# Attention steps in the order turnings, values, masks, scores, with the masks opening the sums

## What is computed

```python
def masked_softmax(s, mask):
    s = jnp.where(mask, s, -jnp.inf)
    m = jnp.max(s, axis=-1, keepdims=True)
    ...
    e = jnp.where(mask, jnp.exp(s - m), 0.0)
    d = jnp.sum(e, axis=-1, keepdims=True)
    return e / jnp.where(d > 0, d, 1.0)
...
    s = jnp.einsum('bqhd,bshd->bhqs', qb, k, preferred_element_type=jnp.float32) * scale
    s = s + (cq[..., :, None] - cum[..., None, :])
    p = masked_softmax(s, kpos[None, :] <= tpos[:, None])
    return jnp.einsum('bhqs,bshd->bqhd', p.astype(v.dtype), v)
```

## Time and profile before

| | |
|---|---|
| median of three runs | 2459.36 us |
| the profiled execution | 2456.09 us |
| its span | 2454.3 us |
| mean granted clock of TensorE | 0.992 |
| TensorE matmuls busy | 2387.1 us, 97% |
| TensorE weight loads busy | 1924.0 us, 78% |
| VectorE busy | 1423.9 us, 58% |
| ScalarE busy | 1019.7 us, 42% |
| GpSimd busy | 274.1 us, 11% |
| chain of waits, by engine | PE 84%, VectorE 7%, issue 5%, ScalarE 3% |

### The profile page before, as it was taken

One profiled execution on the slowest core, in us unless ns is written; L12 is line 12 of the kernel. 1 busy time (PEld: TensorE's weight loads), 2 busy tenths in 40 slices (PEclk: granted clock), 3 DMA queues, 4 the chain that ended last, 5 costly groups with the idle time before them and its releaser, 6 DMA issues.

```text
span 2454.3 us, 32007 instructions
## 1 busy us (share of the span) xinstructions
PE 2387.1 (97%) x12074; PEld 1924.0 (78%) x12086; DVE 1423.9 (58%) x2366; ACT 1019.7 (42%) x1732; POOL 274.1 (11%) x260
## 2 busy tenths in 40 slices
PE   8999899999999999999999999999999999999998
PEld 7877788888887888788888866777888777678886
DVE  3545655655655666566556469947533578676333
ACT  3656654322334444443233334444422354445223
POOL 0000111000000000100000236302100233011001
PEclk9999999999999999999999999999999999999999
DMA  5211002433432111133433312111222221102321
GB/s 196 95 52 44 2 27 95 155 132 117 154 120 95 61 52 61 52 120 132 148 124 137 113 65 73 60 35 36 95 95 95 78 78 61 44 27 78 103 95 52
DMA packets 58039, 211.77 MB, mean 86 GB/s; under 512 B 6432, under 2 KB 6560, under 8 KB 57888
## 3 DMA queue, kind: packets, MB, share of 16 engines
q1 hardware_dynamic: 57456, 208.86, 24.9%
q10 hardware_dynamic: 432, 0.85, 0.1%
HBM read 207.60 MB, written 2.10 MB: 85 GB/s over the span
## 4 chain that ended last, share of the span: by engine, by line
PE 84%; DVE 7%; issue 5%; ACT 3%; POOL 1%; DMA 0%; SPq 0%; ACTq 0%; DVEq 0%; POOLq 0%
PE bank L458 76%; PE last_bank L458 5%; PE bank L468 3%; DVE arena L1145 1%; DVE arena L2232 1%; DVE arena L2234 1%; DVE small L831 1%; ACT arena L819 1%; ACT wparts L566 0%; POOL rstd L625 0%; DMA cb_sb<-cb_dram 0%; DVE arena L2219 0%; DVE arena_r L584 0%; DVE wparts L570 0%; DVE arena L2216 0%
## 5 line engine op out<-in xcount | busy, mean ns | idle before, releaser
L458 PE MATMUL bank<-hT,wparts 128*128 128x512 f32 x5520 | 1330.9, 397 | 5.7 <-DMA cb_sb<-cb_dram 3.5
L458 PEld LDWEIGHTS bank<-hT,wparts 128*128 128x128 f32 x5520 | 1030.4, 189 | 236.5 <-issue 23.2
L570 DVE TENSOR_TENSOR wparts<-ring,wparts 128x1024 fp32r<-128x1024 f32 x290 | 366.8, 1265 | 427.0 <-ACT wparts L566 426.8
L458 PE MATMUL bank<-arena_r,wparts 128*128 128x512 f32 x2400 | 564.0, 395 | 0.0
L458 PEld LDWEIGHTS bank<-arena_r,wparts 128*128 128x128 f32 x2400 | 449.8, 188 | 106.6 <-DVE arena_r L600 0.5
L566 ACT ACTIVATE wparts<-ring 128x1024 fp32r<-128x1024 f32 x332 | 348.2, 1049 | 164.0 <-PE bank L458 131.0
L819 ACT ACTIVATE arena<-bank,small 128x128 f32<-128x128 f32 (+3 forms) x192 | 101.1, 527 | 143.5 <-DVE small L831 142.3
L468 PE MATMUL bank<-cf_sb,arena 128*128 128x128 f32 (+1 forms) x816 | 133.4, 282 | 14.6 <-DMA cf_sb<-cf_dram 4.8
L458 PE MATMUL last_bank<-arena 128*128 128x64 f32 x972 | 131.5, 271 | 8.6 <-DVE arena L854 4.8
L458 PEld LDWEIGHTS last_bank<-arena 128*128 128x128 f32 x972 | 122.6, 193 | 17.5 <-issue 11.3
L831 DVE TENSOR_REDUCE small<-bank 128x1 f32<-128x128 f32 (+3 forms) x192 | 93.4, 486 | 57.1 <-PE bank L458 45.4
(11 more groups left out here) (277 smaller groups left out, 2122.8 us busy)
## 6 DMA issues: line engine op xcount, KB each, us to landing
ring<-weights_dram SPq DMA_DIRECT2D x388, 512.0 KB, 3.4
arena<-x_dram SPq DMA_DIRECT2D x4, 512.0 KB, 5.7
out_dram<-arena SPq DMA_DIRECT2D x4, 512.0 KB, 3.9
rot<-rot_dram SPq DMA_DIRECT2D x1, 512.0 KB, 10.5
rot<-rot_dram ACTq DMA_DIRECT2D x1, 512.0 KB, 3.3
cf_sb<-cf_dram SPq DMA_DIRECT2D x1, 416.0 KB, 8.9
cb_sb<-cb_dram SPq DMA_DIRECT2D x1, 264.0 KB, 9.8
vecs<-vec_dram ACTq DMA_DIRECT2D x1, 258.5 KB, 5.9
```

Of the source, the lines that this page charges most:

```text
L458: i = pe.matmul(*args, **kw)
L570: eng.tensor_tensor(wparts[:, slot, 1, :, :], ring[:, p % RAW, :, :], wparts[:, slot, 0, :, :].bitcast(F32), ALU.subtract)\
```

## The change

In `softmax_maps` TensorE's step i now does, in this order: the turning of map i-3, the values of map i-4, the masks of map i, the scores of map i. The first mask opens the sum (`start=True`), the scores are added to it and the last of them ends it and signals it. A mask of 128 columns opens a sum that is up to 512 wide. Steps are M+4 in place of M+3; ScalarE's and VectorE's copies of the turned map are those of map i-3, VectorE's output that of map i-4. Maximum, exponentials, reciprocal and gate keep their offsets. Within each engine's step, ScalarE, VectorE and GpSimd keep their order. In "fox" the two masks change places, so that the causal one comes first. Pools and lists of numbers stay as they are.

```diff
             def pe_part(pe):
                 for w in ready:
                     pe.wait_ge(*w)
-                for i in range(M + 3):
-                    if i < M and (not together or i % 2 == 0):
...
-                        for j, bank in zip(both, taken):
-                            m = maps[j]
-                            for n, (q, k) in enumerate(m["qk"]):
-                                mm(pe, bank[:, 0:m["width"]], lhsT=q, rhs=k, start=n == 0, stop=False)
-                        for j, bank in zip(both, taken):
-                            extra = maps[j]["masks"]
-                            for n, (a, b, c, w) in enumerate(extra):
-                                for wt in w:
-                                    pe.wait_ge(*wt)
-                                mm(pe, bank[:, c:c + b.shape[-1]], lhsT=a, rhs=b, start=False, stop=n == len(extra) - 1,
-                                   done=(key, "s", j) if n == len(extra) - 1 else None)
-                    if 2 <= i < M + 2:
-                        j = i - 2
+                for i in range(M + 4):
+                    if 3 <= i < M + 3:
+                        j = i - 3
...
-                    if i >= 3:
-                        j = i - 3
+                    if i >= 4:
+                        j = i - 4
...
+                    if i < M and (not together or i % 2 == 0):
...
+                        taken = [banks.take(pe, (key, "s", j), two) for j in both]
+                        for j, bank in zip(both, taken):
+                            for n, (a, b, c, w) in enumerate(maps[j]["masks"]):
+                                for wt in w:
+                                    pe.wait_ge(*wt)
+                                mm(pe, bank[:, c:c + b.shape[-1]], lhsT=a, rhs=b, start=n == 0, stop=False,
+                                   skip_group_check=True)
+                        for j, bank in zip(both, taken):
+                            m = maps[j]
+                            for n, (q, k) in enumerate(m["qk"]):
+                                last = n == len(m["qk"]) - 1
+                                mm(pe, bank[:, 0:m["width"]], lhsT=q, rhs=k, start=False, stop=last, skip_group_check=True,
+                                   done=(key, "s", j) if last else None)
                     yield
...
             def act_part(act):
-                for i in range(M + 3):
-                    if 2 <= i < M + 2 and on_act[i - 2]:
-                        j = i - 2
+                for i in range(M + 4):
+                    if 3 <= i < M + 3 and on_act[i - 3]:
+                        j = i - 3
...
             def dve_part(dve):
-                for i in range(M + 3):
+                for i in range(M + 4):
...
-                    if 2 <= i < M + 2 and not on_act[i - 2]:
-                        j = i - 2
+                    if 3 <= i < M + 3 and not on_act[i - 3]:
+                        j = i - 3
...
-                    if i >= 3:
-                        j = i - 3
+                    if i >= 4:
+                        j = i - 4
...
-                    masks=[(cstb("selneg")[0:96, h:h + 1].to_broadcast([96, P]), parts3[0:96, 0:W], 0, ()),
-                           (identb, cstb("causal"), qt * P, ())],
+                    masks=[(identb, cstb("causal"), qt * P, ()),
+                           (cstb("selneg")[0:96, h:h + 1].to_broadcast([96, P]), parts3[0:96, 0:W], 0, ())],
```

More of the change, by code:

```diff
@@ L800, in pe_part @@
                                stop=(t == n - 1), done=(key, "o", j) if t == n - 1 else None)
+                    if i < M and (not together or i % 2 == 0):
+                        both = (i, i + 1) if together else (i,)
+                        for j in both:
+                            for w in maps[j].get("before", ()):
+                                pe.wait_ge(*w)
+                        taken = [banks.take(pe, (key, "s", j), two) for j in both]
[11 more added lines that the diff above has]
+                                   done=(key, "s", j) if last else None)
                     yield
             def act_part(act):
-                for i in range(M + 3):
-                    if 2 <= i < M + 2 and on_act[i - 2]:
-                        j = i - 2
+                for i in range(M + 4):
+                    if 3 <= i < M + 3 and on_act[i - 3]:
+                        j = i - 3
                         W = maps[j]["width"]
```

## The result

The changed kernel takes 2577.72 us, the median of four runs (2573.94 to 2578.97), against 2459.46 us before: a ratio of 1.048, with an interval of 1.046 to 1.0497. It is 118 us slower where 53 were forecast, and lies outside the stated range. The direction and the loop through VectorE and the one output bank were right; what was missed is mostly the clock.

What follows compares the result with a forecast made beforehand. TensorE was taken as the bound nearly everywhere, the question being whether it stays fed. "nsa" +50, "fox" -2, "dsa" +2 and clock +3 gave +53 us on the median 2459.4, so 2512 us, range 2488 to 2538.

Steps and rivals of the forecast that it cites:

- The loop: "nsa": values wait for VectorE's output, queued behind the newest maximum, through one output bank; 1.46 to 2.83 us per step, +50.
- The sign named for it: "nsa" profile after: values wait for VectorE's output in nearly every step, 0.6 to 1 us each, together about 45 us.
- The clock: TensorE's clock falls a few times in one- and two-tile maps of "nsa": +3 us, bounds 0 and 15.
- the row that held: Earlier profile, 272 to 276 us: clock 1.00 with 2.34 of 4 us busy; the one-tile loop's 58% was likened to it.
- Rival 1: The clock falls for most of "nsa", a third of 64 steps: +25, 2537 us; chance 0.10.
- "dsa": Two layers, pairs of maps: uncovered steps against about half the scores' bank waits saved; +1 us each, bounds -4 and +5 each.
- "fox": Two output banks, so no loop; masks' new place -4.4, last maps +2.5: -2 us, bounds -5 and +5.
- the terms given for the last maps: Last eight maps of "fox": VectorE's copy waits behind the maximum, 0.7 and 1.3 us in turn less 1.2, given as +2.5.
- plain fp32 matmuls don't hold the load up: Mask's weight load behind plain fp32 matmuls like the values doesn't wait; about 0.07 us saved per "fox" step, -4.4 in 64.

Runs made afterwards that it cites:

- filler: Changed kernel plus two bf16 matmuls of 512 columns that compute nothing ahead of each "nsa" turning from step 6 on: 2528.29 us, ratio 1.0289.
- output_late: Kernel before with only VectorE's output in step i made that of map i-4, behind the maximum of map i: 2632.26 us, ratio 1.0714.
- two_out_banks: Changed kernel with "nsa" given two output banks in turn, scores and turnings in banks 3, 4, 5: 2492.54 us, ratio 1.0136.
- out_first: Changed kernel with VectorE's output of map i-4 moved ahead of the maximum of map i: 2504.12 us, ratio 1.0189.
- silu_last: Changed kernel with ScalarE's last copy in "dsa" put ahead of the table load and eleven SiLU activations: 2564.23 us, median of three, ratio 1.0423.
- mask_first: Kernel before with the masks ahead of their scores and the two "fox" masks exchanged, steps cut as before: 2459.70 us, ratio 1.0011.
- early_mask: Kernel before with the masks of map i+1 at the end of step i, behind the values, in "nsa" and "fox": 2457.42 us, ratio 0.9992.

## Why the prediction was wrong

**The loop: right.** Its place, its order and its size at full clock held. "nsa" was to grow by 50 us at full clock and grows by 46.0 in filler; maps 24 to 63 by 33.1 where 36 were forecast, maps 0 to 24 by 12.9 where 14 were (11 and 3). output_late shows that it is VectorE's queue and not TensorE's order, two_out_banks that it is the one bank. The sign named for it, waits of the values of about 45 us together, did not come: in the changed kernel they are 20.5 us in 41 waits from 284 to 440 us, because at half clock TensorE's own work fills more of the time. What the forecast did not see is that the copies, which it had priced inside the first loop only, make a second loop of the same kind. It lies under the first and shows only when that is open: 7.2 and 8.5 us in maps 24 to 63 by two_out_banks and out_first. In maps 0 to 24 these runs are 5.8 and 9.7 us longer than before, part of it falls of the clock (3.4 and 13 us at 0.50).

**The clock: the step that failed.** The prediction took +3 us, bounds 0 and 15, "about the row that held", 2.34 of 4 us busy. Measured are 49.4 us by the medians of the changed kernel and filler; in the profiled executions 44.7 lie in "nsa" and 5.7 in the stretch behind it. The row was no ground for that: it was one stretch of 4 us with busy time around it. In the changed kernel a window of 6.80 us with 4.13 busy, a like share, stands right before the fall. And I priced the fall as one from which TensorE comes back within a few us, as it did in the kernel before. Here it lasts 164 us, and 188 in output_late, though TensorE is then busy 86% of the time. The loop's waits for VectorE do not shrink at half clock (a maximum of 512 columns takes 0.69 us in both), and TensorE's own part nearly doubles (six matmuls of the values 0.85 and 1.51 us). Why the clock stays down that long no run shows; filler shows that it doesn't fall where the waits are filled.

**Rival 1** named this, and priced it at a third of 64 steps, +25; it was 46 of them in one piece, from map 18 on. Its chance of 0.10 was too low. The Trainium skill (TensorE: Matmul & The Clock Gate, "A second HAM failure mode: psum-queue depth-cycling") speaks of a clock that oscillates; the trace shows that only at first, in falls of 3.4 and 6.9 us, and then one stay at 0.50 of 164 us, so the rule pointed to the danger, and not to its form.

**"dsa": +2 forecast, +20 measured**, outside its bounds of 10. Some 5.5 us are the steps themselves. The larger part, 13, is one copy per layer in ScalarE's queue, which the new step count put behind a table load and SiLU (silu_last). The prediction counted waits on TensorE and did not follow where ScalarE's last step falls in the list of numbers.

**"fox": -2 forecast, 0 measured**, of -3.0 in the woven part (-4.4 forecast) and +3.0 in the last maps (+2.5 forecast). The numbers are near, partly by luck: the terms given for the last maps, 0.7 and 1.3 us in turn over eight maps less 1.2, add up to 6.8 and not to 2.5. Putting the masks first is not what gains (mask_first: nothing); putting them behind short matmuls is (early_mask: -3.7). The prediction read from the earlier trace rows that plain fp32 matmuls don't hold the load up; they do in "dsa", where they have up to 512 columns, and the row's have 64. The Trainium skill (TensorE: Matmul & The Clock Gate, "Step-by-step: what each phase is for") has weight loads pulled ahead of running matmuls and tells of no such wait; the idle times of 0.27 us behind the projection and 0.76 in "dsa" speak against it for this load.

**The sum again** with the measured terms: 46.0 for the loop in "nsa", 0 for "fox", 20 for "dsa" and 49.4 for the clock are 115 us of 118. The 20 for "dsa" hold falls of the clock too, such as the 10.3 us behind its last maps. Outside of these stages the profiled execution has 3.4 us more ahead of "nsa", where 17 us stand at 0.50 and 10 did before.

## What to carry to other kernels

When a step on one engine is moved by one, look at the other engines' queues: an output or a copy that comes to stand behind the newest maximum or exponentials makes the whole pipeline wait for the newest score, and with one output bank that wait was paid in nearly every step here. Price such a loop twice, at full clock and at half, before calling it small; if a few idle tenths of a us per step cannot be avoided, a matmul that computes nothing can be worth more than it costs (49 us here). And after changing a step count that other strands are woven with, read where the last steps fall in each queue.

## What the runs showed of the hardware

- TensorE at 0.50 of its clock stayed there for 164 to 188 us while it was 86% busy in a loop with short waits, and rose at 447.3 us, after 6.88 of 7.30 us busy in the first work behind "nsa". With the same loop and 79 matmuls more in maps 24 to 63 it never fell there.
- The load of a bf16 stationary operand waited longer the longer the matmul ahead was: 0, 0.04, 0.16 and 0.27 us behind pairs of fp32r matmuls of 128 to 512 columns, 0.12, 0.33, 0.55 and 0.76 behind plain fp32 ones of the same widths in "dsa", and 0 behind the plain fp32 values of 64 columns. Whether the sum was the same or another made no difference (0.27 behind scores and behind the projection). The scores' fp32r load behind the same projection idled 0.04 in "fox".
- Adding the scores to a bank that a mask of 128 columns had opened cost nothing that the traces show: a pair of 512 columns takes 0.71 us in both orders, at full clock.
